# Expert w1 and w3 with tokens stationary: weights stream 512 wide in three float32r terms, split on ACT, DVE and Pool

## What is computed

```python
def _swiglu(x, w1, w3, w2):
    return (jax.nn.silu(x @ w1) * (x @ w3)) @ w2

def moe_swiglu(x, w_router, b_router, w1, w3, w2):
    logits = (x @ w_router).astype(jnp.float32) + b_router.astype(jnp.float32)
    top_vals, top_idx = lax.top_k(logits, TOP_K)
    top_w = jax.nn.softmax(top_vals, axis=-1)
    gates = jnp.sum(jax.nn.one_hot(top_idx, N_EXPERTS, dtype=jnp.float32) * top_w[..., None], axis=-2)
    out = jnp.zeros_like(x)
    for e in range(N_EXPERTS):
        out = out + gates[..., e:e + 1].astype(x.dtype) * _swiglu(x, w1[e], w3[e], w2[e])
    return out
```

## Time and profile before

| | |
|---|---|
| runs | 2557.40, 2559.49, 2563.46 us; median 2559.49 |
| span of the profiled execution | 2557.7 us |
| TensorE busy | 2456.5 us (96%) |
| DVE, ACT, Pool busy | 1176.2 (46%), 293.8 (11%), 77.4 us (3%) |
| DMA | 524.53 MB, mean 205 GB/s |
| expert stage | from about 864 to 2050 us |

### The profile page before, as it was taken

One profiled execution on the slowest core, in us unless ns is written; L12 is line 12 of the kernel. 1 busy time (PEld: TensorE's weight loads), 2 busy tenths in 40 slices (PEclk: granted clock), 3 DMA queues, 4 the chain that ended last, 5 costly groups with the idle time before them and its releaser, 6 DMA issues.

```text
span 2557.7 us, 38001 instructions
## 1 busy us (share of the span) xinstructions
PE 2456.5 (96%) x16650; PEld 2209.1 (86%) x16650; DVE 1176.2 (46%) x1489; ACT 293.8 (11%) x614; POOL 77.4 (3%) x59
## 2 busy tenths in 40 slices
PE   6999999999999999999999999999999989978999
PEld 6767899987678899999999899999999958646999
DVE  3433677743336344444444444444435420334776
ACT  0123100010231100000000000000000011323000
POOL 2011200000011000000000000000000000100000
PEclk9999999999999899999999999999999997878999
DMA  9533455425224388787878888787878705202440
GB/s 275 197 80 104 159 184 179 151 87 198 102 70 165 125 315 314 287 313 285 312 287 313 291 291 326 276 323 276 324 281 319 266 34 197 65 34 66 165 149 17
DMA packets 270483, 524.53 MB, mean 205 GB/s; under 512 B 10832, under 2 KB 98512, under 8 KB 270192
## 3 DMA queue, kind: packets, MB, share of 16 engines
q1 hardware_dynamic: 268304, 516.77, 56.9%
q0 software_dynamic: 1728, 4.36, 0.9%
q10 hardware_dynamic: 288, 0.91, 0.1%
HBM read 520.95 MB, written 1.05 MB: 204 GB/s over the span
## 4 chain that ended last, share of the span: by engine, by line
PE 93%; DVE 3%; ACT 1%; DMA 1%; issue 1%; SPq 0%; DVEq 0%
PE act_ps L716 44%; PE dve_ps L907 12%; PE act_ps L819 8%; PE dve_ps L819 7%; PE dve_ps L716 7%; PE job_ps L850 5%; PE job_ps L716 2%; PE job_ps L774 2%; PE job_ps L882 1%; DMA weight_ring<-in_w_in 1%; PE job_ps L789 1%; PE act_ps L963 1%; PE job_ps L777 1%; SPq L561 0%; DVE pre_norm L1427 0%
## 5 line engine op out<-in xcount | busy, mean ns | idle before, releaser
L716 PEld LDWEIGHTS act_ps<-arena_mla,weight_ring 128*128 128x128 f32 x7168 | 807.7, 192 | 15.8 <-issue 12.7
L716 PE MATMUL act_ps<-arena_mla,weight_ring 128*128 128x128 f32 x7168 | 810.1, 275 | 9.6 <-issue 8.1
L1677 DVE TENSOR_TENSOR arena_mla<-act_ps,arena_mla 128x512 f32<-128x512 f32 x56 | 38.7, 692 | 489.8 <-PE act_ps L716 489.8
L1657 DVE TENSOR_TENSOR weights_rest<-weight_ring,w_short 128x2048 fp32r<-128x2048 f32 x112 | 256.7, 2292 | 3.8
L1245 ACT ACTIVATE arena_mla<-act_ps 128x512 f32<-128x512 f32 x56 | 33.5, 598 | 1126.6 <-PE act_ps L716 1126.6
L1655 DVE CAST w_short<-weight_ring 128x2048 fp32r<-128x2048 f32 x112 | 137.0, 1223 | 38.5 <-PE dve_ps L907 38.5
L1557 DVE TENSOR_TENSOR weights_rest<-weight_ring,ffn_weights_short 128x2048 fp32r<-128x2048 f32 x66 | 151.3, 2292 | 2.3
L819 PE MATMUL act_ps<-ffn_in_short,ffn_weights_short 128*128 128x256 f32 x480 | 139.6, 291 | 7.3 <-DVE ffn_in_rest L1904 4.5
L907 PE MATMUL dve_ps<-w_short,hidden_short 128*128 128x512 f32 x448 | 143.2, 401 | 0.0
L907 PE MATMUL dve_ps<-weights_rest,hidden_short 128*128 128x512 f32 x448 | 138.2, 390 | 0.0
L907 PE MATMUL dve_ps<-w_short,hidden_rest 128*128 128x512 f32 x448 | 137.9, 389 | 0.0
(11 more groups left out here) (298 smaller groups left out, 3547.2 us busy)
## 6 DMA issues: line engine op xcount, KB each, us to landing
weight_ring<-in_moe_w SPq DMA_DIRECT2D x336, 1024.0 KB, 6.9
weight_ring<-in_w_in SPq DMA_DIRECT2D x44, 1024.0 KB, 7.2
weight_ring<-in_ffn_w SPq DMA_DIRECT2D x32, 1024.0 KB, 6.7
weight_ring<-in_w_out SPq DMA_DIRECT2D x12, 1024.0 KB, 6.3
weight_ring<-in_w_gate SPq DMA_DIRECT2D x11, 1024.0 KB, 5.3
weight_ring<-in_w_up SPq DMA_DIRECT2D x11, 1024.0 KB, 7.8
weight_ring<-in_w_down SPq DMA_DIRECT2D x10, 1024.0 KB, 6.0
weight_ring<-in_w_ple_gate SPq DMA_DIRECT2D x8, 1024.0 KB, 6.5
```

The costliest lines, as they stand in the source:

```text
L716: m = nc.tensor.matmul(out, lhs[k], rhs[k], start=first and k == 0, stop=last and k == len(lhs) - 1)
L1657: V.tensor_tensor(ring_lo[moe_slot(b)][:, half], whole, short, ALU.subtract).then_inc(moe_w2_split, 1)
L1677: V.tensor_tensor(moe_h, act_ps[1][:, 0:GROUP_W], moe_h, ALU.mult).then_inc(moe_h_full, 1)
```

## The change

w1 and w3 get the form that w2 has. Each half block of 128x2048 is a unit, 42 in an expert. ACT makes each unit's rounded copy in one of six buffers, six units ahead of TensorE (`expert_short`); the rest is written over the weights in the ring by Pool for each sixth unit and by DVE for the others (`expert_rest`). The tokens are split too (`x_hi`, `x_lo`, ACT and DVE). TensorE keeps 128x128 of the tokens stationary and streams 512 weight columns, three terms for each of 8 pieces, 24 matmuls a block (`up`). The result has tokens on partitions; after silu and product four transposes turn it (`turn_h`), and the split of h reads the turned bank. The copies to `moe_y` go to ACT. One semaphore, `moe_unit_done`, frees copies and ring slots. The gather is cut in halves, one before each half of w2's last block. In HBM each block is laid out so that a partition's 16 KB are contiguous and each DMA moves 8 KB of it. z goes into job_ps by a product with the identity in place of the zeros; a copy buffer takes its place in memory. The constants' loads on Pool's queue move behind the experts, and a buffer takes their place too. The last expert is peeled off the loops of ACT, DVE and Pool.

```diff
+UNITS = 2 * MOE_BLOCKS
+SHORTS = 6
...
+def by_pool(u):
+    return u % SHORTS == 3
...
+        x_hi = parts("tokens_short", "arena_mla", [P, DT, CAP])
+        x_lo = parts("tokens_rest", "arena_mla", [P, DT, CAP], DT * CAP)
+        h_hi = parts("hidden_short", "arena_gate", [P, 2, 4, CAP])
+        h_lo = parts("hidden_rest", "arena_gate", [P, 2, 4, CAP], 2 * GROUP_W)
+        moe_h = arena_o[:, 1024:1024 + GROUP_W]
+        moe_y = arena_bias[:, 2048:2048 + D]
+        shorts = [parts(f"expert_short{i}", of, [P, 2048], first) for i, (of, first) in enumerate(
+            (("work", 0), ("residual", 0), ("probs", 0), ("pre_norm", 0), ("arena_bias", 0), ("arena_mla", 2048)))]
...
             def load_expert_block(e, b, base):
                 kind, g = MOE_ORDER[b]
+                for c in range(2):
+                    half = slice(c * 2048, (c + 1) * 2048)
+                    sp.dma_start(ring[:, moe_slot(b), half], t[f"moe_{kind}"][e][g][:, half]).then_inc(moe_here[b % SLOTS], 16)
 
...
+            def expert_rest(it, u):
+                slot, half = unit_half(u)
+                pool.wait_ge(moe_w_short, it * UNITS + u + 1)
+                nc.gpsimd.tensor_tensor(ring_lo[slot][:, half], ring[:, slot, half], shorts[u % SHORTS][:, :], ALU.subtract)\
+                    .then_inc(moe_pool_rest, 1)
...
+            experts(0)
...
+            pool.wait_ge(moe_scattered, EXPERTS + 1)
+            pool.dma_start(arena_bias[:, 0:CONST2_N], t["consts2"]).then_inc(const2_loaded, 16)
+            pool.dma_start(arena_bias[:, CONST2_N:CONST2_N + 4 * HD], t["w2_cmp"]).then_inc(const2_loaded, 16)
...
+                def up(it, kind, g, c):
+                    u = moe_unit_of(kind, g, c)
+                    slot, half = unit_half(u)
+                    bank = act_ps[kind == "w3"]
+                    if c == 0 and g >= 1:
+                        pe.wait_ge(moe_silu_done if kind == "w1" else moe_h_done, it * GROUPS_E + g)
+                    if kind == "w1" and g == 0:
+                        pe.wait_ge(moe_x_ready, 2 * (it + turn) + c + 1)
+                    pe.wait_ge(*rest_ready(u, it))
+                    short, rest = tiles(shorts[u % SHORTS][:, :], 4), tiles(ring_lo[slot][:, half], 4)
+                    for k in range(4):
+                        for i, (a, w) in enumerate(((x_hi, short), (x_hi, rest), (x_lo, short))):
+                            m = nc.tensor.matmul(bank[0:CAP, :], a[:, 4 * c + k, :], w[:, k, :], start=(c == k == i == 0),
+                                                 stop=(c == 1 and k == 3 and i == 2))
+                    m.then_inc(moe_unit_done, 1)
...
+                def turn_h(it, g):
+                    pe.wait_ge(moe_h_full, it * GROUPS_E + (g + 1))
+                    for j in range(4):
+                        m = nc.tensor.transpose(act_ps[1][:, j * CAP:(j + 1) * CAP], moe_h[0:CAP, j * P:(j + 1) * P],
+                                                const("ident"))
+                    m.then_inc(moe_h_turned, 1)
...
+                def down(it, g, c):
+                    u = moe_unit_of("w2", g, c)
+                    slot, half = unit_half(u)
+                    if c == 0:
+                        pe.wait_ge(moe_h_done, it * GROUPS_E + (g + 1))
+                        if g == 0:
+                            pe.wait_ge(moe_put_ready, it + turn + 2)
+                    pe.wait_ge(*rest_ready(u, it))
+                    short, rest = tiles(shorts[u % SHORTS][:, :], 2), tiles(ring_lo[slot][:, half], 2)
+                    for k in range(2):
+                        for i, (h, w) in enumerate(((h_hi, short), (h_hi, rest), (h_lo, short))):
+                            for n_half in range(2):
+                                m = nc.tensor.matmul(dve_ps[n_half][0:CAP, :], h[:, g % 2, 2 * c + k, :],
+                                                     w[:, k, n_half * 512:(n_half + 1) * 512], start=(g == c == k == i == 0),
+                                                     stop=(g == GROUPS_E - 1 and c == k == 1 and i == 2))
+                    m.then_inc(moe_unit_done, 1)
+
...
                 with pe.Fori(0, EXPERTS) as e:
                     it = e + base
...
-                            w = tiles(ring[:, moe_slot(b), :], DT)
-                            bank = act_ps[kind == "w3"]
-                            for j in range(4):
-                                m = product(bank[:, j * CAP:(j + 1) * CAP], cols(w, j * P, (j + 1) * P),
-                                            [x_exp[:, k, :] for k in range(DT)])
-                            m.then_inc(moe_h1_ready if kind == "w1" else moe_h3_ready, 1)
-                            if (kind, g) == ("w1", 0):
-                                scatter(it)
-                                for i in range(QT):
-                                    m = nc.tensor.transpose(dve_ps[0][0:CAP, i * P:(i + 1) * P], pick_gate[:, i, :],
-                                                            const("ident"))
-                                m.then_inc(moe_put_turned, 1)
+                            for c in range(2):
+                                down(it, g - 1, c)
+                        turn_h(it, g)
+                    for c in range(2):
+                        gather(it + 1, c)
+                        down(it, GROUPS_E - 1, c)
...
-                        nc.tensor.matmul(acc_ps[b][:, :], const("cos")[0:NOPE, 0:P], consts[0:NOPE, 0:512], start=True, stop=True)
+                        pe.wait_ge(z_summed, b + 1)
+                        m = nc.tensor.matmul(acc_ps[b][:, :], const("ident"), z[:, 2 * b:2 * b + 2, :], start=True, stop=True)
+                    m.then_inc(moe_seeded, 1)
...
+            def expert_short(it, u, free=True):
+                slot, half = unit_half(u)
+                b = u // 2
+                if u % 2 == 0:
+                    act.wait_ge(moe_here[b % SLOTS], 32 * (MOE_TURNS * it + (b // SLOTS + 1)))
+                if free:
+                    act.wait_ge(moe_unit_done, it * UNITS + (u + 1 - SHORTS))
+                nc.scalar.activation(shorts[u % SHORTS][:, :], ring[:, slot, half], ACT.Copy).then_inc(moe_w_short, 1)
...
+                def silu(it, g):
+                    act.wait_ge(moe_unit_done, it * UNITS + (moe_unit_of("w1", g, 1) + 1))
+                    nc.scalar.activation(moe_h[0:CAP, :], act_ps[0][0:CAP, 0:GROUP_W], ACT.Silu).then_inc(moe_silu_done, 1)
+
+                def h_short(it, g):
+                    act.wait_ge(moe_h_turned, it * GROUPS_E + (g + 1))
+                    nc.scalar.activation(h_hi[:, g % 2].rearrange("p f s -> p (f s)"), act_ps[1][:, 0:GROUP_W], ACT.Copy)\
+                        .then_inc(moe_h_short, 1)
+
+                def one(it, last):
+                    for u in range(UNITS):
+                        for g in range(GROUPS_E):
+                            if u == moe_unit_of("w1", g, 1):
+                                silu(it, g)
+                            if u == (4 if g == 0 else moe_unit_of("w2", g - 1, 1)):
+                                h_short(it, g)
+                        if u >= UNITS - 2:
+                            tokens_short(it + (turn + 1), u - (UNITS - 2))
+                        if u == UNITS - 1:
+                            act.wait_ge(moe_unit_done, it * UNITS + UNITS)
+                            for half in range(2):
+                                m = nc.scalar.activation(moe_y[0:CAP, half * 512:(half + 1) * 512], dve_ps[half][0:CAP, :],
+                                                         ACT.Copy)
+                            m.then_inc(moe_y_copied, 1)
+                        ahead = u + SHORTS
+                        if ahead < UNITS:
+                            expert_short(it, ahead)
+                        elif not last:
+                            expert_short(it + 1, ahead - UNITS)
...
+                    act.wait_ge(z_summed, 4)
+                    expert_short(0, 1, free=False)
...
+                    expert_short(0, 2, free=False)
+                    act.wait_ge(moe_seeded, 1)
+                    expert_short(0, 3, free=False)
+                    for half in range(2):
+                        tokens_short(0, half)
+                    for u in (4, 5):
+                        expert_short(0, u, free=False)
                     experts(0)
...
+            def expert_rest(it, u):
+                slot, half = unit_half(u)
+                dve.wait_ge(moe_w_short, it * UNITS + u + 1)
+                V.tensor_tensor(ring_lo[slot][:, half], ring[:, slot, half], shorts[u % SHORTS][:, :], ALU.subtract)\
+                    .then_inc(moe_dve_rest, 1)
...
+                def hidden(it, g):
+                    dve.wait_ge(moe_silu_done, it * GROUPS_E + (g + 1))
+                    dve.wait_ge(moe_unit_done, it * UNITS + (moe_unit_of("w3", g, 1) + 1))
+                    V.tensor_tensor(moe_h[0:CAP, :], act_ps[1][0:CAP, 0:GROUP_W], moe_h[0:CAP, :], ALU.mult)\
```

(63 more changed lines are left out.)

178 lines of the change are left out of this document (72 added, 106 removed).

## The result

The changed kernel takes 2400.33 us (median of four runs, 2397.14 to 2402.32), beside 2558.44 for the kernel before on the same chip: a ratio of 0.9376, 95% interval 0.9359 to 0.9393. The profiled execution has a span of 2398.0 us, where the kernel before had 2557.7. The forecast was 2405 for the median and 2403.6 for the profiled execution.

A forecast was written before the change was run, and what follows sets the result against it. TensorE, busy for 96% of the span, was taken as the bound. 2557.7 - 800.2 + 611.5 + 24.6 + 10 (stalls) = 2403.6 us profiled, 2405 for the median; own range 2385 to 2425, range 2385 to 2475 with most of rival 1.

The forecast's parts named there:

- Removed and added: TensorE over 56 groups: 800.2 us of w1 and w3 removed; 611.5 of new matmuls and 24.6 of transposes added.
- the 17 us up or 10 down that line 819 left open: w1 and w3 matmuls staying in one PSUM bank: excess per matmul adds 17 us, or no bank switch gains some 10.
- The length of an expert: One expert on TensorE falls by 19.1 us, from 146.9 to 127.8, with 1.5 us of small gaps left as they are.
- The stall before w2's last block: Each expert's last group: TensorE waits 1.3 us for the rest of h; 8 experts, 10 us (0 to 25).
- the y copies on ACT: End of each expert: copying y moves from DVE to ACT, 2 x 0.60 us instead of 2 x 0.69, counted as nothing.
- The placing by hand: From T, the end of w2's last unit: Pool T+3.0 to 7.5, h rest done T+20.3; exclusion hidden, barely.
- the exclusive load: DVE and Pool never overlapping in a group: 12.8 + 4.5 = 17.4 us, against TensorE's 16.83.
- Transfers: Expert weight loads: 390 GB/s or more, 16.1 us a group, hidden; 374 GB/s needed in a group.
- Entry: Start of the expert stage: DVE's first rest precedes the router, tokens pass by halves; net 0 us, from -2 to +5.
- The shared port: Rival 1: DVE and Pool exclude each other, a group is 17.37 us; 2435, up to 2499; chance 0.26.
- rivals 2 to 4: 2: transfers bind, 2491, chance 0.09. 3: HBM layout slows transfers, 3005, 0.05. 4: tokens stationary brings no pace, 2680, 0.01.
- rival 4: w1 and w3's 48 matmuls take 0.39 us each, line 907's mean duration, not its pitch: slower, 2680; chance 0.01.

The follow-up runs named there:

- the kernel with two terms: The changed kernel without the third term of w1 and w3 (32 matmuls a group instead of 48), Pool's rest kept: 2363.12 us, ratio 0.9232.
- the two-term kernel: At 423 GB/s: the changed kernel without the third term of w1 and w3, all rests on DVE, none on Pool: 2288.94 us, ratio 0.8942.

## Why the prediction was right

**What bounds.** Held. Busy share and chain were TensorE's, and with less TensorE work the time fell by that work: 159.7 us of span.

**Removed and added.** A group was to go from 19.75 to 16.83 and went to 16.81. In parts: w1 and w3 10.93 for 10.92 (0.2278 a matmul, so one bank or two makes no difference, and the 17 us up or 10 down that line 819 left open are both out); w2 5.44 for 5.46; transposes 0.44 for 0.45, 0.11 each as in the earlier trace rows. Over 56 groups 164.6 us, where the sum had 164.1. The rule to read the distance of matmuls and not their mean duration held as well: line 951's records have a mean of 0.39 us, and by that the kernel would have been slower.

**The length of an expert.** 126.9 for 127.8. 7 x 16.81 + 3.56 (gather) + 3.67 (scatter and two transposes) + 1.5 (waits) = 126.4, so the small gaps, which I had left at 1.5 us an expert, are 0.5. That term was mis-sized, and the 0.9 us that an expert is shorter, seven times, are 6.3 of the difference; the sum of 2403.6 was 5.6 over the span of 2398.0. The waits of TensorE in the kernel before, 895 to 2045 us, show where most of the 1.5 was:

```profile
PE act_ps L716 <- issue: 8.1, 7, 3.3
```

At each of the seven passages to a new expert TensorE stood before w1's first product, six times 0.6 to 0.9 us and once 3.3, released by nothing that the profile shows (the earlier trace rows have the 8.1 too). The changed kernel has no such wait. Why it went is not shown.

**The stall before w2's last block.** I had 1.3 us for 8 experts, 10 in all, at one place. The rows have 5.8 there (0.8 each) and 4.8 at another, the transposes, 10.6 in all. The forecast of 10 us was right by luck. At the first place I costed DVE's rests by their duration, 2.29, where they follow each other at 2.20 (three of them begin at 1415.89 and the product at 1424.74: 8.85, of which Pool held 2.3), so the rest of h was ready at T+19.7 and not T+20.3; TensorE asks at T+19.0. The second place I had missed. Some 3.1 of its 4.8 us are the y copies on ACT, put at nothing: together with two table loads they stand ahead of the silu, and with them on DVE these waits are gone. The other 1.8 are the first expert's; they outlast that edit (2.8 there), and their cause stays open.

**DVE and Pool.** The placing by hand held. With T = 1410.69 in the changed kernel, Pool and DVE ran so (timeline, 1410 to 1436 us):

```profile
1413.64 4.62 POOL L688 TENSOR_TENSOR weights_rest<-weight_ring,expert_short 128x2048 fp32r<-128x2048 f32 x1 [16.16 <-ACT expert_short L1324]
...
1415.89 8.93 DVE L1768 TENSOR_TENSOR weights_rest<-weight_ring,expert_short 128x2048 fp32r<-128x2048 f32 x3 [3.04 <-ACT expert_short L1324]
1424.74 0.68 DVE L1793 TENSOR_TENSOR arena_o<-act_ps,arena_o 128x512 f32<-128x512 f32 x1
...
1429.75 0.68 DVE L1798 TENSOR_TENSOR hidden_rest<-act_ps,hidden_short 128x512 fp32r<-128x512 f32 x1
```

Pool starts at T+2.95 (placed at 3.0) and ends at T+7.57 (7.5); the rest of h ends at T+19.7 (20.3). The sum of the exclusive load was wrong: not 17.4 against TensorE's 16.83, but 5 x 2.20 + 4.5 = 15.5 against 16.81. Two errors were in it: durations for distances, and the small operations counted as port users. By that sum "hidden, barely" had 1.3 us a group of room instead of -0.5; by the kernel with two terms, whose group the port bounds at 16.03 us, it is 0.8. The Trainium skill (SBUF — State Buffer, Who interferes with whom) says that a DVE instruction with two SBUF inputs contends with a GpSimd one that reads SBUF, that the shared ports are an exclusive lock, and that issue order decides who blocks. The runs agree for the subtract as well (5.64 and 6.08 on Pool, three rests in 10.45 on DVE).

**Transfers.** Hidden, as forecast, and with more room than I gave them: 423 GB/s in the two-term kernel, where I took 390. The Trainium skill (DMA: Bandwidth & Descriptors, Specifications) puts a core's share of HBM at about 358 GB/s, while its section Measured (HBM→SBUF, 128 partitions, SWDGE, issued from GpSimd) has 425 GB/s for a large transfer with the neighbouring core idle. This case's 423 over 58 us agrees with the second and is over the first.

**Entry.** 0 was forecast, from -2 to +5, for when the weights' matmuls begin: 870.15 after 871.00. Inside it two things I had not seen cancel out. The gather began 1.0 us later, at 865.13; DVE's and Pool's timelines of the changed kernel show why:

```profile
857.89 4.50 POOL L688 TENSOR_TENSOR weights_rest<-weight_ring,expert_short 128x2048 fp32r<-128x2048 f32 x1 [48.31 <-ACT expert_short L1324]
858.48 3.94 DVE L1759 TENSOR_SCALAR arena_o<-arena_o 128x18 f32<-128x18 f32 x1
```

18 columns on DVE took 3.94 us, where the kernel before has 0.17, because Pool's first rest held the port until 862.39; the gather waited 7.0 us for DVE's picks, before 3.28. With no rest on Pool it began at 863.63. And the first half of the tokens is ready after half a gather, which takes back 1.85.

**The rivals.** The shared port was the right thing to fear: it is what the stage meets next, 0.8 to 1.3 us a group away. But it didn't bind here, and nor did rivals 2 to 4.

**Two slips in the recorded sums.** (1910.2 - 0.1 - 881.7)/7 is 146.91 and not 146.94; nothing hangs on it. The 2680 of rival 4 adds 56 x 4.95 us to the forecast instead of to the time before; its own terms give 2559 + 277 = about 2840. That changes neither the direction nor the chance of that rival.

## What to carry to other kernels

Cost a stream of instructions on any engine by the distance between their starts, on VectorE too: a tenth of a microsecond each, and the small operations that don't use the port, turned a group with 0.8 to 1.3 us of room into one that seemed 0.5 too long. Count on a shared port only the operations that need it, and then ask whether the second engine is wanted at all: here the changed kernel gained 3 to 6 us and the two-term one 74 when Pool's work went to DVE. When a step that costs nothing for its own engine is moved, look at what is queued behind it: 1.2 us of copies on ACT stood, with two table loads, ahead of an expert's first silu, and TensorE waited 0.5 us each time.

## What the hardware showed that I had not expected

A tiny DVE operation can pay for a long one of Pool: 128x18 took 3.94 us. The picks of each expert (line 1778, 128x128 from SBUF to SBUF) have a median of 0.34 us and a mean of 0.86, with a maximum of 1.62; with no rest on Pool their maximum is 0.35. The products and rests of h, which read PSUM, take at most 0.70 us in every kernel.

ACT loads its table twice at the head of each expert but the last (the changed kernel, ACT's timeline, 1508 to 1512 us):

```profile
1508.31 1.28 ACT L1324 ACT_TABLE_LOAD   x1
...
1509.61 1.92 ACT L1324 ACTIVATE expert_short<-weight_ring 128x2048 fp32r<-128x2048 f32 x1
1511.54 1.28 ACT L1337 ACT_TABLE_LOAD   x1
```

The next operation follows 0.02 us after the first load has ended (1509.59), and the second load 0.01 after that (1511.53): 1.28 us each and nothing more. The Trainium skill (ScalarE: Activation LUTs, What ACT_TABLE_LOAD costs) has 1283 ns for the load, which agrees, and 1380 ns for a drain with it, of which these rows show nothing.

One core's 16 DMA engines moved 423 GB/s over 58 us with rows of 8 KB; the most that the rows of before show is 390 over 7 us.
